# RWKV-7 scan in a one-core diffusion step: keys without zero padding, A and B made head by head on 64-row halves of TensorE, and the state as the padded operand

## The reference, cut to what matters

```python
def rwkv7_scan(r, w, k, v, kk, a, s0):
    def step(s, inp):
        r_t, w_t, k_t, v_t, kk_t, a_t = inp
        sa = jnp.einsum('bhvk,bhk->bhv', s, -kk_t)
        s = s * w_t[:, :, None, :] + sa[..., None] * (kk_t * a_t)[:, :, None, :] + v_t[..., None] * k_t[:, :, None, :]
        return s, jnp.einsum('bhvk,bhk->bhv', s, r_t)
    xs = tuple(jnp.moveaxis(z, 1, 0) for z in (r, w, k, v, kk, a))
    s_fin, o = lax.scan(step, s0.astype(F32), xs)
    return jnp.moveaxis(o, 0, 1), s_fin
```

## Time and profile before

| | |
|---|---|
| median of three runs | 3084.23 us (3070.08 to 3104.94) |
| span of the profiled execution, first to last instruction | 3100.0 us |
| PE busy, share of the span | 84% |
| DVE, ACT busy | 40%, 25% |
| mean granted TensorE clock | 0.902 of full speed |
| the scan, from its first A tile to the last `OT` | 1495.7 to about 2617 us |

### The profile page before, as it was taken

The page is one execution under the profiler, slowest core; times in us unless marked ns, Lnnn a source line. Parts: engine busy times, 40 slices in busy tenths (PEclk is TensorE's granted clock), DMA queues, the critical chain, the costliest instruction groups (busy, mean ns, idle before and its releaser), DMA issues.

```text
span 3100.0 us, 35206 instructions
## 1 busy us (share of the span) xinstructions
PE 2596.5 (84%) x14506; PEld 1969.5 (64%) x14506; DVE 1236.9 (40%) x2688; ACT 785.9 (25%) x1570; POOL 158.7 (5%) x178
## 2 busy tenths in 40 slices
PE   6999905488899835997799999999999998968974
PEld 3544705455566523556688889888888887556653
DVE  2254126622111116100666665666566665221104
ACT  2253212302011102001334343344243342020111
POOL 2000003400100010001000000000000000000001
PEclk9999956688899967999899997999899999969987
DMA  6144180005699732221000000000000000048962
GB/s 222 55 136 155 56 352 4 2 16 181 232 324 325 229 138 91 68 68 53 3 3 1 1 3 1 1 1 3 1 1 1 3 1 35 28 154 272 346 210 108
DMA packets 202299, 300.99 MB, mean 97 GB/s; under 512 B 12180, under 2 KB 170112, under 8 KB 201760
## 3 DMA queue, kind: packets, MB, share of 16 engines
q1 hardware_dynamic: 180096, 225.62, 22.1%
q0 software_dynamic: 11984, 40.63, 3.5%
q10 hardware_dynamic: 10064, 32.51, 2.6%
HBM read 237.39 MB, written 61.35 MB: 96 GB/s over the span
## 4 chain that ended last, share of the span: by engine, by line
PE 75%; DVE 12%; ACT 3%; DMA 3%; issue 2%; ACTq 2%; POOL 2%; SPq 0%; POOLq 0%; DVEq 0%
PE psum_ring L677 68%; PE psum_ring L1013 4%; DMA arena<-expert_inputs 1%; PE psum_ring L767 1%; ACTq L1263 1%; ACT h_normed L1158 1%; ACTq L1260 1%; ACT arena L1351 1%; DVE arena L1991 1%; DVE x_resid L1991 1%; DVE x_resid L2004 1%; DVE arena L2004 1%; POOL arena L633 1%; POOL expert_inputs L621 1%; DVE h_normed L1829 1%
## 5 line engine op out<-in xcount | busy, mean ns | idle before, releaser
L677 PE MATMUL psum_ring<-arena 128*128 128x64 f32 (+4 forms) x5200 | 982.4, 339 | 54.6 <-ACT arena L1173 17.5
L677 PEld LDWEIGHTS psum_ring<-arena 128*128 128x128 f32 (+1 forms) x5200 | 762.2, 197 | 214.6 <-issue 132.5
L677 PE MATMUL psum_ring<-x_resid 128*128 128x64 f32 x2368 | 334.2, 281 | 0.0
L677 PEld LDWEIGHTS psum_ring<-x_resid 128*128 128x128 f32 x2368 | 306.4, 199 | 0.0
L677 PE MATMUL psum_ring<-arena,weight_ring 128*128 128x512 f32 (+1 forms) x832 | 230.3, 438 | 5.6 <-DVE arena L1804 3.4
L677 PE MATMUL psum_ring<-h_normed,weight_ring 128*128 128x512 f32 (+1 forms) x768 | 211.7, 437 | 5.8 <-ACT h_normed L1158 5.8
L677 PEld LDWEIGHTS psum_ring<-arena,weight_ring 128*128 128x128 f32 x832 | 127.9, 193 | 107.4 <-issue 102.6
L677 PEld LDWEIGHTS psum_ring<-h_normed,weight_ring 128*128 128x128 f32 x768 | 117.8, 192 | 98.9 <-issue 98.8
L677 PE MATMUL psum_ring<-weight_ring,small 128*2 128x256 f32 x768 | 171.9, 382 | 0.0
L677 PE MATMUL psum_ring<-h_normed 128*128 128x128 f32 x190 | 43.4, 411 | 117.5 <-DVE h_normed L1829 98.0
L677 PEld LDWEIGHTS psum_ring<-weight_ring,small 128*2 128x2 f32 x768 | 63.7, 85 | 108.6 <-issue 15.3
(11 more groups left out here) (346 smaller groups left out, 3316.8 us busy)
## 6 DMA issues: line engine op xcount, KB each, us to landing
arena<-in_moe_w SPq DMA_DIRECT2D x105, 1024.0 KB, 11.2
weight_ring<-in_w_mod SPq DMA_DIRECT2D x48, 1024.0 KB, 5.4
arena<-expert_inputs SPq DMA_DIRECT2D x35, 512.0 KB, 8.1
expert_outputs<-arena POOLq DMA_DIRECT2D x32, 512.0 KB, 7.8
weight_ring<-in_ab_w_in SPq DMA_DIRECT2D x14, 1024.0 KB, 5.0
expert_inputs<-arena ACTq DMA_DIRECT2D x1, 12800.0 KB, 36.8
expert_outputs<-arena ACTq DMA_DIRECT2D x1, 12800.0 KB, 67.3
weight_ring<-in_ab_w_out SPq DMA_DIRECT2D x4, 1024.0 KB, 6.4
```

Of the source, the lines that this page charges most:

```text
L677: return nc.tensor.matmul(out, lhsT, rhs, start=start, stop=stop)
```

## The change

The padding moves from the keys to the state. `RHS4_0/1` (4 x 128 columns per pair) become `KR_0/1` (2 x 128 columns per pair: decayed KK and decayed query, both heads above each other, no zeros), filled by two 128-partition instructions in place of four 64-partition ones. A and B are made head by head: each head of a pair is one matmul over its own 64 partitions, 256 columns wide, in place of one 512-column matmul for the pair over 128. The first head of every pair writes the first bank of the tile, the second head the second bank, so the tile's columns stand as (head, pair) and no longer (pair, head); the masks read them in that order and write SBUF in the old one. `R0` grows to 128 columns per pair with the two heads' states on the diagonal and zeros elsewhere, so that RHS and OT take one 128-column product per pair, in place of one 64-column product for each head. In OT it now stands first. On DVE, making `R0` and scaling it into `ST` become two 64-partition instructions each. GpSimd clears the two `R0` in place of the four `RHS4`.

```diff
@@ PE: A and B @@
+            def head_products(ps, left, right):
+
+                for j in range(UC):
+                    for hh in range(2):
+                        pr = slice(HD * hh, HD * hh + HD)
+                        c0 = 512 * hh + 256 * j
+                        ins = mm(ps[:, c0:c0 + 256], left[pr, j * P:(j + 1) * P], right[pr, 256 * j:256 * j + 256])
+                return ins
...
-                    rh = f"RHS4_{(g * NCH + st) % 2}"
+                    kr = f"KR_{(g * NCH + st) % 2}"
...
-                        for j in range(UC):
-                            ins = mm(ps[:, 512 * j:512 * j + 512], z["BE"][:, j * P:(j + 1) * P],
-                                     z[rh][:, 512 * j:512 * j + 512])
-                        done(ins)
+                        done(head_products(ps, z["BE"], z[kr]))
...
@@ PE: RHS @@
-                            if st:
-                                mm(out, z[rh][:, hl * 256:hl * 256 + P], z["R0"][:, (hl // 2) * HD:(hl // 2 + 1) * HD],
-                                   True, False)
-                            ins = mm(out, z["BR"][:, hl * 256:hl * 256 + P], V1[:, ch, hv], st == 0, True)
+                            j, hh = divmod(hl, 2)
+                            if st and hh == 0:
+                                mm(ps[:, j * P:(j + 1) * P], z[kr][:, j * 256:j * 256 + P],
+                                   z["R0"][:, j * P:(j + 1) * P], True, False)
+                            ins = mm(out, z["BR"][:, hl * 256:hl * 256 + P], V1[:, ch, hv], st == 0, st == 0 or hh == 1)
...
@@ PE: OT, in the loop over the heads hl @@
+                            j, hh = divmod(hl, 2)
+                            if st and hh == 0:
+                                mm(ps[:, j * P:(j + 1) * P], z[kr][:, j * 256 + P:(j + 1) * 256],
+                                   z["R0"][:, j * P:(j + 1) * P], True, False)
+                            mm(out, z["BR"][:, hl * 256 + P:(hl + 1) * 256], V1[:, ch, hv], st == 0, False)
                             ins = mm(out, z["AR"][:, hl * 256 + P:(hl + 1) * 256], z["U"][:, hl * HD:(hl + 1) * HD],
-                                     False, st == 0)
-                            if st:
-                                ins = mm(out, z[rh][:, hl * 256 + P:(hl + 1) * 256],
-                                         z["R0"][:, (hl // 2) * HD:(hl // 2 + 1) * HD], False, True)
+                                     False, st == 0 or hh == 1)
...
@@ DVE: decayed_operands @@
-                for hh in range(2):
-                    pr = slice(HD * hh, HD * hh + HD)
-                    TT(r5[pr, :, hh, 0, :], c3(z["KK"])[pr], c3(z["E3"])[pr], ALU.mult)
-                    ins = TT(r5[pr, :, hh, 1, :], R1[pr, cg, ts], c3(z["E1"])[pr], ALU.mult)
-                ins.then_inc(S["unit_ready"], 1)
+                kr = z[f"KR_{(g * NCH + st) % 2}"].rearrange("p (j a t) -> p j a t", j=UC, a=2)
+                TT(kr[:, :, 0, :], c3(z["KK"]), c3(z["E3"]), ALU.mult)
+                TT(kr[:, :, 1, :], R1[:, cg, ts], c3(z["E1"]), ALU.mult).then_inc(S["unit_ready"], 1)
...
@@ DVE: masks, A as B @@
-                        free(TT(z["AR"].rearrange("p (h c) -> p h c", c=256),
-                                ps.rearrange("p (h c) -> p h c", c=256), m, ALU.mult), n)
+                        free(TT(by_half(z["AR"]), in_banks(ps), mask, ALU.mult), n)
...
@@ DVE: the state into R0, and back into ST behind OT @@
-                            TT(STR[d]["R0"].rearrange("p (j v) -> p j v", v=HD),
-                               ST[:, KT * d + UC * g:KT * d + UC * (g + 1), :],
-                               em[:, par + 2 * d:par + 2 * d + 2].unsqueeze(2).broadcast_to([P, UC, HD]),
-                               ALU.mult).then_inc(S["r0_ready"], 1)
+                            for hh in range(2):
+                                pr = slice(HD * hh, HD * hh + HD)
+                                ins = TT(r0[pr, :, HD * hh:HD * hh + HD],
+                                         ST[pr, KT * d + UC * g:KT * d + UC * (g + 1), :],
+                                         em[pr, par + 2 * d:par + 2 * d + 2].unsqueeze(2).broadcast_to([HD, UC, HD]),
+                                         ALU.mult)
+                            ins.then_inc(S["r0_ready"], 1)
...
-                            link(TT(ST[:, KT * d + UC * g:KT * d + UC * (g + 1), :], r0,
-                                    eb.unsqueeze(2).broadcast_to([P, UC, HD]), ALU.mult))
+                            for hh in range(2):
+                                pr, vs = slice(HD * hh, HD * hh + HD), slice(HD * hh, HD * hh + HD)
+                                ins = TT(ST[pr, KT * d + UC * g:KT * d + UC * (g + 1), :], r0[pr, :, vs],
+                                         eb[pr].unsqueeze(2).broadcast_to([HD, UC, HD]), ALU.mult)
+                            link(ins)
```

More of the change, by code:

```diff
@@ L649, in _ @@
             for d in range(2):
-                for q in range(2):
-                    nc.gpsimd.memset(STR[d][f"RHS4_{q}"], 0.0).then_inc(S["rw_clear"], 1)
+                nc.gpsimd.memset(STR[d]["R0"], 0.0).then_inc(S["rw_clear"], 1)
             nc.gpsimd.memset(Hf[:, :], 0.0).then_inc(S["rw_clear"], 1)
@@ L994, in _ @@
                         ps = open_tile(T["BR" + u] + d)
[L995 to L998, removed]
+                        done(head_products(ps, z["KP"], z[kr]))
                     for d in range(2):
@@ L1880, in _ @@
             read_out(dve, T["stT"] + 1)
-            dve.wait_ge(S["rw_clear"], 6)
+            dve.wait_ge(S["rw_clear"], 4)
             def c3(a):
@@ L1980, in _, with by_half, in_banks, causal @@
             idb = ident.unsqueeze(1).broadcast_to([P, HG, P])
+            def by_half(a):
+                return a.rearrange("p (j h c) -> p h j c", h=2, c=256)
+            def in_banks(a):
+                return a.rearrange("p (h j c) -> p h j c", h=2, c=256)
+            def causal(d):
+                m = CO[:, C_RMASK + 256 * d:C_RMASK + 256 * d + 256]
+                return m.unsqueeze(1).unsqueeze(1).broadcast_to([P, 2, UC, 256])
             for g in range(NGRP):
@@ L1989, in _ @@
                         ps = full(dve, n)
-                        m = CO[:, C_RMASK + 256 * d:C_RMASK + 256 * d + 256].unsqueeze(1).broadcast_to([P, HG, 256])
-                        free(TT(z["AR"].rearrange("p (h c) -> p h c", c=256),
-                                ps.rearrange("p (h c) -> p h c", c=256), m, ALU.mult), n)
+                        mask = causal(d)
+                        free(TT(by_half(z["AR"]), in_banks(ps), mask, ALU.mult), n)
                         read_out(dve, n)
@@ L2002, in _ @@
                         ps = full(dve, n)
-                        m = CO[:, C_RMASK + 256 * d:C_RMASK + 256 * d + 256].unsqueeze(1).broadcast_to([P, HG, 256])
-                        free(TT(z["BR"].rearrange("p (h c) -> p h c", c=256),
-                                ps.rearrange("p (h c) -> p h c", c=256), m, ALU.mult), n)
+                        mask = causal(d)
+                        free(TT(by_half(z["BR"]), in_banks(ps), mask, ALU.mult), n)
                     for d in range(2):
@@ L2065, in _ @@
                         tt = ps[:, 512:512 + UC * P].rearrange("p (j c) -> p j c", c=P)
[L2066 removed]
+                        r0 = z["R0"].rearrange("p (j c) -> p j c", c=P)
                         eb = em[:, par + 2 * d:par + 2 * d + 2]
@@ L2069, in _ @@
                             for hh in range(2):
-                                pr = slice(HD * hh, HD * hh + HD)
-                                ins = TT(r0[pr], r0[pr], tt[pr, :, HD * hh:HD * hh + HD], ALU.add)
+                                pr, vs = slice(HD * hh, HD * hh + HD), slice(HD * hh, HD * hh + HD)
+                                ins = TT(r0[pr, :, vs], r0[pr, :, vs], tt[pr, :, vs], ALU.add)
                             link(ins)
-                            link(TT(ST[:, KT * d + UC * g:KT * d + UC * (g + 1), :], r0,
-                                    eb.unsqueeze(2).broadcast_to([P, UC, HD]), ALU.mult))
+                            for hh in range(2):
+                                pr, vs = slice(HD * hh, HD * hh + HD), slice(HD * hh, HD * hh + HD)
+                                ins = TT(ST[pr, KT * d + UC * g:KT * d + UC * (g + 1), :], r0[pr, :, vs],
+                                         eb[pr].unsqueeze(2).broadcast_to([HD, UC, HD]), ALU.mult)
+                            link(ins)
                         else:
```

8 lines of the change are left out of this document (3 added, 5 removed).

## The result

The changed kernel takes **3404.72 us** (median of three runs, 3368.9 to 3438.04) against 3084.23 before: a ratio of 1.0986, 95% interval 1.0897 to 1.1076. The forecast was 3380 us. The profiled execution is the fastest of its three (3368.9 us, span 3366.8), so spans differ by 267 us where medians differ by 320.

What follows compares the result with a forecast made beforehand. Each step was taken as bound by DVE for some 9.6 us and PE for some 45; -28.6 + 4.6 + 360 - 39.6 = +296 us on the 3084 us median gave 3380 us, range 3050 to 3540 (forecast's own 3240 to 3480).

Steps and rivals of the forecast that it cites:

- The halves: A and B on 64-row halves of PE run side by side, taking 3.5 to 4.4 us instead of 6.9.
- They are worth next to nothing in themselves: PE's 2.5 to 3.4 us gained in A and B become waiting, as DVE's 9.6 us chain stays late.
- The state's products: RHS and OT lose 16 instructions a step on PE's part of the chain: 1.79 us a step, 28.6 us saved.
- DVE's second instruction: Scaling the state into ST behind OT takes a second DVE instruction, open for direction 1: 0.29 x 16 = 4.6 us added.
- The masks: DVE's masks of A and B read 1024 columns in another order, unchanged at 1.22 us; range allows 8 us in all.
- The falls: PE's gaps behind B let the clock fall just ahead of the levels in every step: 18 x 20 = 360 us.
- the 22 places elsewhere: Places in the trace before where PE had as little work and the clock fell to 1.2 GHz within a few microseconds.
- not side by side: Rival: the halves run one after another, A and B stay near 6.9 us, 3060 us in all; chance 0.14.
- clock holds: Rival: halves side by side, PE's gaps behind B free under DVE's chain, 3060 us; chance 0.07.
- brief falls: Rival: the clock falls but returns within the second level, 5 us a step, 3120 us; chance 0.09.
- Low through all levels: Rival: the clock stays low through all levels, 25 us a step, 500 us, giving 3520 us; chance 0.14.
- an even chance between two lengths of a low: Size of a fall in the levels: early return or wholly low equally likely, (25 + 11) / 2 = 18 us a step.

Runs made afterwards that it cites:

- experiment 4: Kernel of Experiment 1 with the state's products in RHS and OT back to one 64-column product per head: 3109.09 us, ratio 1.0014.
- Experiment 1: Changed kernel with B's products made three times into the same tile, filling PE's gap: 3100.82 us, ratio 0.9997 to the kernel before.
- experiment 3: Kernel before without pair 1's products of A and B, masks reading pair 0's twice (output wrong): 3451.99 us against 3113.95 before.
- experiment 7: Changed kernel reordered: B's products behind M0 of direction 0, B's masks, R0 and decay sums later on DVE: 3035.58 us, ratio 0.9763.
- Experiment 10: Kernel before with decay sums behind G4's masks and ACT's second logs and square behind level 4's copies of N: 3071.47 us, ratio 0.9892.
- experiment 12: experiment 7 with ACT's second logs and square, exponentials, and DVE's sums, centring and direction 0's operands moved later: 3008.77 us, ratio 0.9778.

## Why the prediction was right

**The halves** side by side: predicted 3.5 to 4.4 us, measured 3.7. **They are worth next to nothing in themselves**: DVE's chain was predicted at 9.6 to 9.9 us; from its first addition behind `OT` (2678.59) to `M0` of d = 1 (2688.51) it is 9.9 us; PE's waits are 1.45 and 1.58 us, up to 1.9 predicted. That DVE waits for A's first tile at no point holds for the step that the prediction read and not for all. Behind the steps of group 0, where no norm stands ahead of the next mask, and behind the context step of each later group it does wait in before. One such row:

```profile
1606.31 1.23 DVE L1991 TENSOR_TENSOR arena<-psum_ring,consts 128x1024 f32<-128x1024 f32 x1 [0.41 <-PE psum_ring L677]
```

Eight waits of 0.40 to 1.04 us make 4.8 us in all, and 0.6 us of them are left in the changed kernel: a gain of some 4 us at most that the prediction put at nothing.

**The state's products**: 1.79 us a step, exactly, shown twice (the chain above, and experiment 4). **DVE's second instruction**: 0.29 us; making `R0` and the decayed operands stayed hidden (a clean step changed by 1.49 and those two terms make 1.50). **The masks** cost the same in their new order.

The mean clock is 0.803, 0.81 predicted. **The falls** were the largest term and the one with the thinnest ground, the 22 places elsewhere. Experiment 1 shows the cause by taking the gap away, experiment 3 by making it without the halves. The rule of the Trainium skill, TensorE: Matmul & The Clock Gate, "Why this matters for your kernels", speaks of longer idle gaps only; here 1.45 and 1.58 us with short transposes between them are enough, and the measurement decides. The rivals "not side by side", "clock holds" and "brief falls" are refuted. "Low through all levels" is refuted as a rule: the 19 steps of the profiled execution range from 57 to 81 us (one of 36.5 at the start of the scan aside), and seven stay within 67.

**Its size.** The 19 intervals, 1293.5 us, less clean ones of experiment 1's length (its 1023.6 us less some 29 for its own falls: 995) leave 299 us of falls. The last step, from its gate tile to the end of `OT`, takes 113.3 us where before takes 87.8: 25.5 more although its clean length is 1.5 less, so 27 us of falls. Together 326 us or 16.3 a step, where the prediction put 360 and 18. With it the sum for the profiled execution is -24 + 326 - 40 = +262; 267 was measured, and the other 5 us were not traced. So the term was a tenth too high for this execution. The median run was 36 us longer, at a mean clock of 0.792, and has no trace. The 18 us a step rested on an even chance between two lengths of a low, not on a count, so that the forecast was within 25 us of the median is partly luck.

**What the prediction did not see** is that before itself had a loose 0.9 us in level 4, by two queues late together, and that its four falls in the scan all began right behind it. It took before's falls, 39.6 us, as given.

## What to carry to other kernels

When an edit shortens work that hides under another engine's chain, ask what TensorE does in the time it wins: if it waits there between short pieces, the clock may fall and cost many times the gain in the narrow work behind. Try needed dense work in the gap, or right behind it, before idle products. And where an engine waits for "issue", look at every semaphore of the instruction: clear all queues that are late together, and judge by like steps of the profile, not by medians that a chance fall moves by 30 us.

## What the hardware showed that I had not expected

All eight lows at `M0` that met B's products in experiment 7 were over in 3.4 us (0.75, then 0.91 and 1.00 in successive stretches of 5 us in the one shown), while the lows at `M0` ahead of 64-column levels last 14 to 68 us in the changed kernel. Dense work is not the only thing that goes with a short low: the eight behind `D4` in the same trace ended as soon without it.

In every trace the falls that did not begin at `M0` began 15.3 to 16.2 us behind the gate tile, where a single wait of 0.6 to 0.9 us in a run of 64-column products ends or up to 2.3 us behind it, and in some steps only. In the trace with that wait at 0.38 us there was none. Experiment 10's trace has none either at 0.81 us. So the wait most likely starts these falls and does not force them; experiment 12 moved other work too, so this is not shown by one edit alone.

A fall of the kind in experiment 1 (2180 to 2200), windows:

```profile
2170.00:2180.00 10.00, 8.82 (x79) 8.71 (x80) 5.17 (x14) 7.28 (x17) 0.00 (x0) 1.00 0.01 2
2180.00:2190.00 10.00, 10.00 (x53) 10.00 (x52) 5.24 (x15) 2.32 (x6) 0.00 (x0) 0.52 0.00 0
2190.00:2200.00 10.00, 10.00 (x49) 9.94 (x49) 5.59 (x17) 2.78 (x6) 0.00 (x0) 0.50 0.01 2
2200.00:2210.00 10.00, 10.00 (x88) 10.00 (x87) 3.66 (x12) 1.54 (x4) 0.00 (x0) 0.95 0.00 0
```

PE shows 8.82 us busy in the ten ahead of the fall and is full while it lasts, at half speed: 53 and 49 instructions where 79 and 88 stand on either side.
